# Chunked attention on one Trainium2 core: one 256-column matmul for each key tile, with an fp32 folding matmul behind it

## What is computed

```python
scores = jnp.einsum("bcqhd,bckhd->bhcqk", qc, kb).astype(jnp.float32) * (dh ** -0.5)
scores = scores + rel_bias_band(rel_bias).astype(jnp.float32)[None, :, None]
scores = jnp.where((key_chunk >= 0)[None, None, :, None, :], scores, -jnp.inf)
probs = jax.nn.softmax(scores, axis=-1).astype(v.dtype)
out = jnp.einsum("bhcqk,bckhd->bcqhd", probs, vb)
```

## Time and profile before

| what | value |
|---|---|
| median of 3 runs | 2591.8 us |
| profiled execution | 2588.12 us, span 2586.3 us |
| this attention stage | about 1225 to 1484 us of the span |
| granted TensorE clock, whole span | 0.988 |
| VectorE busy | 1496.9 us (58%) |
| ScalarE busy | 812.3 us (31%) |
| GpSimd busy | 203.6 us (8%) |

### The profile page before, as it was taken

One profiled execution on the slowest core, in us unless ns is written; L12 is line 12 of the kernel. 1 busy time (PEld: TensorE's weight loads), 2 busy tenths in 40 slices (PEclk: granted clock), 3 DMA queues, 4 the chain that ended last, 5 costly groups with the idle time before them and its releaser, 6 DMA issues.

```text
span 2586.3 us, 32814 instructions
## 1 busy us (share of the span) xinstructions
PE 2497.3 (97%) x12758; PEld 2079.0 (80%) x12758; DVE 1496.9 (58%) x2068; ACT 812.3 (31%) x1387; POOL 203.6 (8%) x116
## 2 busy tenths in 40 slices
PE   8998999999999999998999999998999999999998
PEld 6786878888888888787888888877788888888886
DVE  5675464344444447546444488887576464646466
ACT  2374331011011102536443365554522121212022
POOL 4313200000000000002222200100000000000000
PEclk9999999999999999998999999998999999999999
DMA  4406223232233223113110001021012020202011
GB/s 125 37 17 90 66 72 91 86 95 79 81 97 95 73 77 120 37 37 118 43 36 25 25 17 34 17 98 41 17 58 73 25 73 24 73 24 73 24 57 74
DMA packets 201577, 157.08 MB, mean 61 GB/s; under 512 B 56184, under 2 KB 176512, under 8 KB 201472
## 3 DMA queue, kind: packets, MB, share of 16 engines
q1 hardware_dynamic: 183344, 124.94, 16.6%
q10 hardware_dynamic: 18128, 30.71, 4.7%
HBM read 147.23 MB, written 11.56 MB: 61 GB/s over the span
## 4 chain that ended last, share of the span: by engine, by line
PE 87%; DVE 5%; ACT 3%; DMA 2%; issue 2%; SPq 0%; POOL 0%; ACTq 0%; DVEq 0%; POOLq 0%
PE pd L851 25%; PE pd L853 25%; PE pd L852 25%; PE pt L1381 1%; PE pd L1436 1%; PE pd L1350 1%; PE pt L1451 1%; DMA raw<-in_w_out 1%; PE pt L1398 1%; PE pt L871 1%; DMA raw<-in_w_ff 1%; PE pt L1400 1%; PE pt L1471 1%; PE pt L1470 1%; PE pt L1469 1%
## 5 line engine op out<-in xcount | busy, mean ns | idle before, releaser
L851 PE MATMUL pd<-actT_hi,st_hi 128*128 128x512 f32 x1872 | 746.7, 399 | 7.0 <-DVE st_lo L2303 3.3
L853 PE MATMUL pd<-actT_hi,st_lo 128*128 128x512 f32 x1872 | 732.0, 391 | 0.0
L852 PE MATMUL pd<-actT_lo,st_hi 128*128 128x512 f32 x1872 | 731.8, 391 | 0.0
L851 PEld LDWEIGHTS pd<-actT_hi,st_hi 128*128 128x128 f32 x1872 | 353.4, 189 | 77.6 <-ACT evac L1616 3.7
L853 PEld LDWEIGHTS pd<-actT_hi,st_lo 128*128 128x128 f32 x1872 | 352.9, 189 | 75.6
L852 PEld LDWEIGHTS pd<-actT_lo,st_hi 128*128 128x128 f32 x1872 | 353.8, 189 | 65.8
L851 PE MATMUL pd<-mv_hi,hid_hi 128*128 128x512 f32 x864 | 337.0, 390 | 3.1 <-DVE acc L2608 1.5
L853 PE MATMUL pd<-mv_hi,hid_lo 128*128 128x512 f32 x864 | 336.2, 389 | 0.0
L852 PE MATMUL pd<-mv_lo,hid_hi 128*128 128x512 f32 x864 | 336.2, 389 | 0.0
L1766 ACT ACTIVATE mv_hi<-raw 128x1024 fp32r<-128x1024 f32 x54 | 55.9, 1056 | 604.7 <-PE pd L853 477.9
L1616 ACT ACTIVATE evac<-pd 128x1024 f32<-128x1024 f32 x76 | 77.9, 1025 | 452.1 <-PE pd L853 452.1
(11 more groups left out here) (349 smaller groups left out, 3721.3 us busy)
## 6 DMA issues: line engine op xcount, KB each, us to landing
raw<-in_w_ff SPq DMA_DIRECT2D x64, 512.0 KB, 4.0
ada_raw<-in_w_ada ACTq DMA_DIRECT2D x64, 384.0 KB, 3.2
raw<-in_w_up SPq DMA_DIRECT2D x44, 512.0 KB, 3.8
raw<-in_w_in SPq DMA_DIRECT2D x30, 512.0 KB, 3.8
raw<-in_w_down SPq DMA_DIRECT2D x22, 512.0 KB, 3.2
acc<-in_x SPq DMA_DIRECT2D x16, 512.0 KB, 8.8
raw<-in_w_out SPq DMA_DIRECT2D x12, 512.0 KB, 3.2
raw<-in_w_ple_gate SPq DMA_DIRECT2D x8, 512.0 KB, 3.8
```

The source lines that it names most:

```text
L851: pe.matmul(out_ap, a_hi, b_hi, start=start, stop=False, skip_group_check=check)
L852: pe.matmul(out_ap, a_hi, b_lo, start=False, stop=False, skip_group_check=check)
L853: return pe.matmul(out_ap, a_lo, b_hi, start=False, stop=stop, skip_group_check=check)
```

## The change

For each key tile there is now one matmul: the stationary operand is v hi beside v lo of the head (128 columns, so `v` is stored as `[P, RT, 2, P]` with hi in columns 0:64 and lo in 64:128), and the moving operand is the turned probabilities, hi beside lo (256 columns, `pT2` as `[P, 2, 2, NA]`). The result is turned: features on partitions (hi rows above lo rows), queries on columns, 128 for hi probabilities and 128 for lo ones. Three operations follow each step: ScalarE copies the lo columns to `o_sum` (`out_low`), VectorE adds the hi columns (`out_add`), and a plain fp32 matmul with `o_sum` as weights and the 128x64 matrix `fold` (two identities, one below the other) turns it back and adds the hi and lo rows (`fold2`), into the upper half of the same bank. `head_out` is left with the reciprocal and one multiplication; it is moved ahead of `low2` and one iteration later.

```diff
@@ outputs2, and the new fold2 (PE)
-                o = pt[:, hh, (qt % 4) * P:(qt % 4 + 1) * P]
+                o = pt[:, hh, 0:2 * P].rearrange("p (a n) -> p a n", n=P)
                 for j in range(n):
-                    kt = qt - n + 1 + j
-                    pe.matmul(o.rearrange("p (a b) -> p a b", b=64), pT2_hi[:, z % 2, j * P:(j + 1) * P],
-                              v[:, kt, :, hh, :], start=j == 0, stop=False, skip_group_check=True)
-                    last = pe.matmul(o[:, 0:64], pT2_lo[:, z % 2, j * P:(j + 1) * P], v[:, kt, 0, hh, :],
-                                     start=False, stop=j == n - 1, skip_group_check=True)
+                    last = pe.matmul(o, v[:, qt - n + 1 + j, hh, :], pT2[:, z % 2, :, j * P:(j + 1) * P],
+                                     start=j == 0, stop=j == n - 1, skip_group_check=True)
                 last.then_inc(pv_done, 1)
+            def fold2(z):
+                _, hh, qt, _ = step2(z)
+                pe.wait_ge(o_added, z + 1)
+                pe.matmul(fold_bank(hh)[:, qt % 4, :], o_sum[:, z % 2, :], fold[:, :], start=True, stop=True,
+                          skip_group_check=True).then_inc(o_folded, 1)
             scores2(0)
-            for z in range(N2 + 2):
+            for z in range(N2 + 3):
...
-                if z >= 2:
+                if 2 <= z < N2 + 2:
                     outputs2(z - 2)
+                if z >= 3:
+                    fold2(z - 3)
@@ ScalarE
+            def out_low(z):
+                act.wait_ge(pv_done, N1 + z + 1)
+                if z >= 2:
+                    act.wait_ge(o_folded, z - 1)
+                act.activation(o_sum[:, z % 2, :], pt[:, z % 2, P:2 * P], ACT.Copy).then_inc(o_low, 1)
+            for z in range(N2 + 3):
                 if 2 <= z < N2 + 2:
                     parts2(z - 2)
+                if z >= 3:
+                    out_low(z - 3)
@@ VectorE
+            def out_add(z):
+                dve.wait_ge(o_low, z + 1)
+                dve.tensor_tensor(o_sum[:, z % 2, :], pt[:, z % 2, 0:P], o_sum[:, z % 2, :], ALU.add)\
+                    .then_inc(o_added, 1)
             def head_out(g):
-                dve.wait_ge(pv_done, N1 + 16 * pair + 8 * half + 6 + hh + 1)
+                dve.wait_ge(o_folded, 16 * pair + 8 * half + 6 + hh + 1)
...
                 link(dve.reciprocal(rinv[:, c], den[:, c]))
-                o = pt[:, hh, :].rearrange("p (b n) -> p b n", n=P)
-                link(dve.tensor_copy(o_out, o[:, :, 0:64]))
-                link(dve.tensor_tensor(o_out, o_out, o[:, :, 64:P], ALU.add))
+                link(dve.tensor_tensor(o_out, fold_bank(hh), rinv[:, c].unsqueeze(2).to_broadcast([P, 4, 64]),
+                                       ALU.mult))
                 dve.sem_inc(o_half, 1)
-                last = dve.tensor_tensor(o_out, o_out, rinv[:, c].unsqueeze(2).to_broadcast([P, 4, 64]), ALU.mult)
...
+            link(dve.tensor_tensor(fold[:, :], ident[:, 0:64], ident[:, 64:P], ALU.add))
             mask_bias(0)
             mask_bias(1)
             for z in range(N2 + 4):
                 if z < N2:
                     top2(z)
+                g = half2_ended(z - 4)
+                if g is not None:
+                    head_out(g)
                 if 2 <= z < N2 + 2:
                     low2(z - 2)
+                if 3 <= z < N2 + 3:
+                    out_add(z - 3)
                 if 1 <= z <= N2:
                     q, part = 1 + (z - 1) // 16, ended(PLAN_A[(z - 1) % 16])
                     job_lo(0, 4 * NJ1 + NJ2 * q, att2[q % 2], part, q, one=True)
-                g = half2_ended(z - 3)
-                if g is not None:
-                    head_out(g)
```

More of the change, by code:

```diff
@@ L154, in qkv_set @@
                 k=(place(f"k_hi{name}", [P, S], F32R, kv_at), place(f"k_lo{name}", [P, S], F32R, kv_at + 4 * KB)),
-                v=place(f"v{name}", [P, RT, 2, 2, 64], F32R, kv_at + 8 * KB))
+                v=place(f"v{name}", [P, RT, 2, P], F32R, kv_at + 8 * KB))
         q1 = [(place(f"q_a1{n}", [P, S], F32R, at), place(f"q_b1{n}", [P, S], F32R, at + 4 * KB))
@@ L207, in build @@
         prob2 = place("prob2", [P, 2, NA], F32, R_B)
-        pT2_hi = place("pT2_hi", [P, 2, NA], F32R, R_B + 5 * KB)
-        pT2_lo = place("pT2_lo", [P, 2, NA], F32R, R_B + 10 * KB)
+        pT2 = place("pT2", [P, 2, 2, NA], F32R, R_B + 5 * KB)
+        fold = place("fold", [P, 64], F32, R_A + 28 * KB)
+        o_sum = place("o_sum", [P, 2, P], F32, R_A + 29 * KB)
         bias2 = [place(f"bias2{b}", [P, 2, NA], F32, R_B + (15 + 5 * b) * KB) for b in range(2)]
@@ L291, in build @@
         o_half = sem("o_half")
+        o_low = sem("o_low")
+        o_added = sem("o_added")
+        o_folded = sem("o_folded")
         s_small = sem("s_small")
@@ L433, in half2_ended, with fold_bank @@
             return z // 16 * 4 + z % 16 // 8 * 2 + z % 2 if 0 <= z < N2 and z % 8 >= 6 else None
+        def fold_bank(hh):
+            return pt[:, hh, 2 * P:HB].rearrange("p (b n) -> p b n", n=64)
         def half_ended(z):
@@ L1466, in outputs3 @@
                 for j in range(nt):
-                    v_hi, v_lo = v[:, kt0 + j, 0, hh, :], v[:, kt0 + j, 1, hh, :]
+                    v_hi, v_lo = v[:, kt0 + j, hh, 0:64], v[:, kt0 + j, hh, 64:P]
                     w_hi, w_lo = wt_hi[:, z % 2, j * P:(j + 1) * P], wt_lo[:, z % 2, j * P:(j + 1) * P]
@@ L1658, in job_hi @@
                     elif kind == "T":
-                        act.activation(kv["v"][:, 4 * half:4 * half + 4, 0, :, :],
+                        act.activation(kv["v"][:, 4 * half:4 * half + 4, :, 0:64],
                                        src.rearrange("p (r h c) -> p r h c", h=2, c=64), ACT.Copy).then_inc(jb_hi, 1)
@@ L1916, in parts2 @@
                     act.wait_ge(pv_done, N1 + z - 1)
-                act.activation(pT2_hi[:, z % 2, 0:n], ptT[:, 0:n], ACT.Copy).then_inc(pt_hi_s, 1)
-            for z in range(N2 + 2):
+                act.activation(pT2[:, z % 2, 0, 0:n], ptT[:, 0:n], ACT.Copy).then_inc(pt_hi_s, 1)
+            def out_low(z):
[4 more added lines that the diff above has]
+            for z in range(N2 + 3):
                 if 2 <= z < N2 + 2:
                     parts2(z - 2)
+                if z >= 3:
+                    out_low(z - 3)
                 if 1 <= z <= N2:
@@ L2165, in job_lo @@
                     else:
-                        v = kv["v"][:, 4 * half:4 * half + 4, :, :, :]
-                        dve.tensor_tensor(v[:, :, 1, :, :], src.rearrange("p (r h c) -> p r h c", h=2, c=64),
-                                          v[:, :, 0, :, :].bitcast(F32), ALU.subtract).then_inc(jb_lo, 1)
+                        v = kv["v"][:, 4 * half:4 * half + 4, :, :]
+                        dve.tensor_tensor(v[:, :, :, 64:P], src.rearrange("p (r h c) -> p r h c", h=2, c=64),
+                                          v[:, :, :, 0:64].bitcast(F32), ALU.subtract).then_inc(jb_lo, 1)
             def value_lo(j):
@@ L2472, in low2 @@
                 dve.wait_ge(pt_hi_s, N1 + z + 1)
-                dve.tensor_tensor(pT2_lo[:, z % 2, 0:n], ptT[:, 0:n], pT2_hi[:, z % 2, 0:n].bitcast(F32),
+                dve.tensor_tensor(pT2[:, z % 2, 1, 0:n], ptT[:, 0:n], pT2[:, z % 2, 0, 0:n].bitcast(F32),
                                   ALU.subtract).then_inc(pt_lo_s, 1)
+            def out_add(z):
+                dve.wait_ge(o_low, z + 1)
+                dve.tensor_tensor(o_sum[:, z % 2, :], pt[:, z % 2, 0:P], o_sum[:, z % 2, :], ALU.add)\
+                    .then_inc(o_added, 1)
             def head_out(g):
                 pair, half, hh = g // 4, g // 2 % 2, g % 2
-                dve.wait_ge(pv_done, N1 + 16 * pair + 8 * half + 6 + hh + 1)
+                dve.wait_ge(o_folded, 16 * pair + 8 * half + 6 + hh + 1)
                 c = slice(8 * hh + 4 * half, 8 * hh + 4 * half + 4)
@@ L2483, in head_out @@
                 link(dve.reciprocal(rinv[:, c], den[:, c]))
-                o = pt[:, hh, :].rearrange("p (b n) -> p b n", n=P)
-                link(dve.tensor_copy(o_out, o[:, :, 0:64]))
-                link(dve.tensor_tensor(o_out, o_out, o[:, :, 64:P], ALU.add))
+                link(dve.tensor_tensor(o_out, fold_bank(hh), rinv[:, c].unsqueeze(2).to_broadcast([P, 4, 64]),
+                                       ALU.mult))
                 dve.sem_inc(o_half, 1)
-                last = dve.tensor_tensor(o_out, o_out, rinv[:, c].unsqueeze(2).to_broadcast([P, 4, 64]), ALU.mult)
                 if g % 4 == 3:
-                    last.then_inc(o_done, 1)
-                else:
-                    link(last)
+                    dve.sem_inc(o_done, 1)
+            link(dve.tensor_tensor(fold[:, :], ident[:, 0:64], ident[:, 64:P], ALU.add))
             mask_bias(0)
```

## The result

The changed kernel takes 2609.09 us, the median of 4 runs (2608.07 to 2612.90), against 2592.06 us before. The ratio is 1.0069, with a 95% interval of 1.0057 to 1.0081: 17.0 us slower (14.8 to 21.0), where 15.5 were forecast. In a second session, in which the kernel before took 2593.81 us, the same kernel took 2608.31 us: a ratio of 1.0052 (1.0037 to 1.0068), 14.5 us. The profiled execution has a span of 2607.9 us.

What follows compares the result with a forecast made beforehand. PE's order of work was taken to set the time. Waits 16.8, k job 1.0 and drain 1.1 less 3.4 gained make 15.5 us slower: 2591.8 + 15.5 = 2607.3 us, 8-in-10 range 2597 to 2622 us.

Steps and rivals of the forecast that it cites:

- The wait at head_out: At iterations 2, 3, 10 and 11, PE stands still before turn2 while low2 queues behind head_out on VectorE: 16.8 us lost.
- PE's own work: In outputs2 and fold2, a tile costs 0.117 us instead of 0.222 and a fold 0.20: 3.4 us gained over four pairs.
- the four iterations with little projection work: Iterations 13 to 16: the chain turn2, top2, low2 sets the pace, so less PE work gains nothing.
- The clock: Rival, 18%: TensorE's clock also falls behind the long waits at iterations 10 and 2, 12 us more: 2619 us.
- A window at half clock behind a wait: Sign that the forecast is wrong: half-clock windows behind turn2 at iterations 2 and 10.
- The k job behind head_out: At iteration 11, the k job's lo part follows head_out, low2 and out_add; PE waits about 0.25 us, four times: 1.0 us.
- The drain: At the stage's end, five products and two folds at lower clock, with head_out and out_add between folds: 1.1 us more.
- The wait for out_add between the folds: At the drain, PE waits between the folds for 0.99 us of head_out, 0.28 of out_add and 0.15.
- The rule on pairs of a load and a 128-column matmul: About 81 ns per pair: a tile would cost 0.162 us before the change, gaining 0.045 us rather than 0.105.
- the 0.111 us of the earlier trace: Measured cost of one weight load in the kernel before, given as 0.11 us; each further key tile takes two, 0.222 us.

Runs made afterwards that it cites:

- late head_out: The changed kernel with head_out moved behind low2 in VectorE's order, nothing else: 2588.74 us, ratio 0.9992 to the kernel before.
- second profile: The changed kernel run once more, unaltered, and profiled again: 2608.31 us.
- the kernel before with the wait in it: The kernel before with its own four-operation head_out put ahead of low2 in the same VectorE iteration, no fold or new matmul: 2638.13 us, ratio 1.0187.

## Why the prediction was right

**The wait at head_out: forecast 16.8 us, measured 17.0.** The changed kernel against the one with the late head_out, iteration by iteration: 5.98 - 4.01 = 1.97 us at iteration 10 and 6.04 - 5.40 = 0.64 at iteration 11, four times; 5.16 - 3.72 = 1.44 and 4.73 - 3.97 = 0.76 at iterations 2 and 3, three times; together 17.0. The forecast had 1.96, 0.78, 1.42 and 0.53. The bracket says 1.80 and not 1.97, because idle time counts from the modelled end of the last matmul (1339.13) and the distance from the start of the fold: 1338.80 to 1340.93 is 2.13 us, where the transposes otherwise follow after 0.17.

**PE's own work: forecast a gain of 3.4 us, measured 5.1.** The step was right, its size too small. By n, a pair's iterations gained -0.10 and -0.13 us (n = 1; forecast -0.18), -0.03 twice (-0.07), 0.09 and 0.06 (0.03), 0.24 and 0.14 (0.14), and for n = 5 0.28, 0.34, 0.17 and 0.34 (0.25). Where n is 4 or 5, iterations with scores behind the fold gained 0.10 to 0.17 us more than iterations 10 and 12, with transposes behind it. The fold itself follows 0.12 us behind the last product and is followed after 0.17 us, not 0.20. That the four iterations with little projection work would gain nothing came out to 0.03 us each, with one exception: in the last pair iteration 14 took 2.97 us with the new products and 2.63 before (2.98 with the late head_out), a loss of 0.35 us that the sum did not have and no run explains.

**The clock: a rival with 18%, which happened behind one of the 14 head_out waits of the first profile** and behind none of the second. A window at half clock behind a wait was one of the prediction's signs of being wrong, and its sum had put the clock at nothing. It cost 1.6 us (262.23 against 260.64 us), not the 12 us of the rival, which had it at every long wait.

**The k job behind head_out: forecast 1.0 us, measured 0.1 us at each of four iterations 12**, some 0.35 us in all (4.32 against 4.22 in the second pair). This term was three times too large. **The drain: forecast 1.1 us, measured 0.3** (from the last turn2 to the next stage's scores 4.95 us against 4.66). That step failed in its condition: it took PE at its lower clock for the five products and both folds. In the windows of the changed kernel the granted clock was still 1.00 up to 1505 us, and 0.79 from 1505 to 1506:

```profile
1502.50 0.85 PE L1405 MATMUL pt<-pT,v2b 128*128 128x256 f32 x5 [0.89 <-DVE pT L2495]
1503.18 0.33 PE L1413 MATMUL pt<-fold,o_sum 128*128 128x64 f32 x2
...
1504.35 0.29 DVE L2500 TENSOR_TENSOR o_sum<-pt,o_sum 128x128 f32<-128x128 f32 x1 [0.16 <-DVE rows L2511]
1504.70 0.43 PE L1413 MATMUL pt<-fold,o_sum 128*128 128x64 f32 x2 [1.18 <-DVE o_sum L2500]
1505.06 0.33 PE L1450 MATMUL pd<-k_hi2a,q_hi2a 64*128 64x128 f32 x2
```

The wait for out_add between the folds is there as described, 1.18 us.

**The sum.** In the stage 17.0 for the waits, 1.6 for the clock, 0.3 for the k job and 5.1 less for the products make 13.8 us, which is the difference of the two profiles; 0.3 for the drain makes 14.1. Without the fall of the clock, as in the second profile, it is 12.5. The medians are 17.0 and 14.5 us apart, so 2 to 3 us are left, which would lie outside the stage. Behind it the profiles of the two kernels agree (from the next stage's scores to the end 1102.7 us before, 1102.8 and 1103.8 changed); ahead of it they scatter by 14 us over the nine profiles, and no run here gives the rest to the change or takes it from it.

The wait, which carries the forecast, was right in mechanism and in size. That the total of 15.5 us lies so close is in part luck: the products gained 1.7 us more than forecast and the k job and the drain cost 1.4 us less, which by themselves make 12.5 us; the fall of the clock and the 2 to 3 us outside the stage, none of them in the sum, brought the measured time back up.

The rule on pairs of a load and a 128-column matmul (the Trainium skill, TensorE: Matmul & The Clock Gate, Back-to-back issue gap) would have made the gain of the products less than half as large. On the 160 tiles that set the pace, 0.045 us each is an estimate of 7.2 us, less than the 9.6 us of 48 folds at 0.20 us, so the late head_out would be slower than the kernel before in the stage. It is 5.1 us faster, so the 0.111 us of the earlier trace rows was the number to take.

## What to carry to other kernels

When an operation that waits for the end of another engine's iteration is moved ahead of one that the other engine needs to begin its next, the whole way through is paid, whatever the share of busy time says: VectorE was busy for 120.19 of the 262.23 us of the stage and still held PE for 17 us. Look at what stands between the producer and the waiter on the bound engine; if it is nothing, put the drain last in the order, and if it must come early, move other work of the bound engine in between. And judge a cheaper instruction only where its engine sets the pace: here 16 of 64 steps could give nothing, until work from elsewhere was put there.

## What was not expected of the hardware

How long PE waited did not decide by itself whether TensorE's granted clock fell to its 1.2 GHz level. In the kernel before with the wait in it, it fell behind the waits of 2.16 and 2.06 us, 8 us apart, at all three pair boundaries, where transposes and few products stand ahead of them; but behind the waits of 2.72 us, which have projection work around them, in one case of four, and behind those of 1.64 us, also in one of four. The wait of 1.80 us of the changed kernel had a fall behind it in one pair of eight (two profiles). Eight of the nine falls cost 1.5 to 1.7 us by the distances, the longest 2.8. What decides it was not tested. And a plain fp32 matmul with 64 moving columns costs 0.17 to 0.22 us, two weight loads, the same as one with a single column in the earlier trace rows.
